# Head sums of squares of nine query and key tiles: one fp32 matmul, or two rounded passes over high and low parts

## What is computed

```python
def rms_norm_2(x, g):
    xf = x.astype(jnp.float32)
    y = xf * lax.rsqrt(jnp.mean(xf * xf, axis=-1, keepdims=True) + EPS)
    return (y * g.astype(jnp.float32)).astype(x.dtype)

    qa = apply_axial_rope_2(rms_norm_2(qa, q_gain), *rope_axial)
    ka = apply_axial_rope_2(rms_norm_2(ka, k_gain), *rope_axial)
```

## Time and profile before

| | |
|---|---|
| median of 3 runs | 2500.09 us (2498.11 to 2503.15) |
| the profiled execution, its own time | 2499.82 us |
| its span, first to last instruction | 2497.6 us |
| PE busy | 2438.6 us (98%) |
| POOL busy | 1639.5 us (66%) |
| DVE busy | 1101.5 us (44%) |
| ACT busy | 668.8 us (27%) |
| mean granted TensorE clock | 0.996 |

### The profile page before, as it was taken

The page is one execution under the profiler, slowest core; times in us unless marked ns, Lnnn a source line. Parts: engine busy times, 40 slices in busy tenths (PEclk is TensorE's granted clock), DMA queues, the critical chain, the costliest instruction groups (busy, mean ns, idle before and its releaser), DMA issues.

```text
span 2497.6 us, 32448 instructions
## 1 busy us (share of the span) xinstructions
PE 2438.6 (98%) x11606; PEld 1976.9 (79%) x11606; DVE 1101.5 (44%) x1465; ACT 668.8 (27%) x1252; POOL 1639.5 (66%) x1431
## 2 busy tenths in 40 slices
PE   7999999999999999999999999999999999999998
PEld 4886678888888887778888888888888787788886
DVE  4454654454333227865333223333226666433311
ACT  4264521112111106652111101111112774211100
POOL 3554856666666776546666776667777775666775
PEclk9999999999999999999999999999999999999999
DMA  6314533233232332003232332333333222232332
GB/s 267 114 59 145 173 114 98 95 96 98 92 101 92 104 107 87 28 13 109 92 101 92 101 109 94 100 93 100 101 104 110 80 74 65 85 100 93 101 101 84
DMA packets 68802, 248.03 MB, mean 99 GB/s; under 512 B 7408, under 2 KB 9968, under 8 KB 68080
## 3 DMA queue, kind: packets, MB, share of 16 engines
q1 hardware_dynamic: 63808, 232.81, 29.4%
q10 hardware_dynamic: 4912, 14.12, 1.5%
HBM read 244.80 MB, written 2.10 MB: 99 GB/s over the span
## 4 chain that ended last, share of the span: by engine, by line
PE 92%; DVE 3%; ACT 2%; issue 1%; POOL 1%; DMA 1%; DVEq 0%; ACTq 0%; POOLq 0%
PE pb L541 72%; PE pb L1098 4%; PE pb L1038 2%; PE pb L806 2%; PE pb L962 2%; PE pb L550 1%; PE pb L740 1%; PE pb L709 1%; PE pb L1081 1%; PE pb L1066 1%; PE pb L1054 1%; PE pb L944 1%; ACT tb L1345 1%; PE pb L928 1%; PE pb L691 1%
## 5 line engine op out<-in xcount | busy, mean ns | idle before, releaser
L541 PE MATMUL pb<-ar,w_hi 128*128 128x512 f32 x5312 | 1644.8, 391 | 3.6 <-DVE ar L1911 2.7
L541 PEld LDWEIGHTS pb<-ar,w_hi 128*128 128x128 f32 x5312 | 995.1, 188 | 222.1 <-issue 8.1
L541 PE MATMUL pb<-ar,w_lo 128*128 128x512 f32 x2656 | 1034.2, 389 | 0.0
L394 POOL TENSOR_TENSOR w_lo<-raw,w_hi 128x1024 fp32r<-128x1024 f32 x380 | 952.1, 2505 | 31.7
L541 PEld LDWEIGHTS pb<-ar,w_lo 128*128 128x128 f32 x2656 | 499.0, 188 | 103.9
L391 POOL TENSOR_TENSOR still<-still 128x1 f32<-128x1 f32 x393 | 81.3, 207 | 693.4 <-PE pb L541 550.8
L392 POOL TENSOR_SCALAR w_hi<-raw 128x1024 fp32r<-128x1024 f32 x380 | 403.7, 1062 | 0.0
L1986 DVE TENSOR_TENSOR tb<-pb,nb 128x512 f32<-128x512 f32 x88 | 60.9, 692 | 400.8 <-PE pb L541 400.8
L1992 DVE TENSOR_TENSOR ar<-tb,ar 128x512 f32 x88 | 156.2, 1775 | 90.9 <-ACT ar L1416 90.9
L1416 ACT ACTIVATE ar<-tb 128x512 f32 x88 | 55.7, 633 | 512.8 <-DVE tb L1989 512.8
L1893 DVE SCALAR_TENSOR_TENSOR x<-pb,x 128x512 f32<-128x512 f32 x48 | 36.2, 755 | 344.2 <-PE pb L541 339.8
(11 more groups left out here) (257 smaller groups left out, 2396.9 us busy)
## 6 DMA issues: line engine op xcount, KB each, us to landing
raw<-wstream SPq DMA_DIRECT2D x428, 512.0 KB, 3.6
raw<-wstream SPq DMA_DIRECT2D x4, 1024.0 KB, 10.7
x<-xt ACTq DMA_DIRECT2D x2, 2048.0 KB, 9.8
tb<-wstream SPq DMA_DIRECT2D x2, 1024.0 KB, 11.7
rt<-wstream SPq DMA_DIRECT2D x2, 1024.0 KB, 11.9
out<-x ACTq DMA_DIRECT2D x8, 256.0 KB, 2.2
rt<-nbias ACTq DMA_DIRECT2D x4, 384.0 KB, 3.8
nb<-nbias ACTq DMA_DIRECT2D x4, 384.0 KB, 3.6
```

The costliest lines, as they stand in the source:

```text
L394: pool.tensor_tensor(lo, src, hi.bitcast(F32), ALU.subtract).then_inc(s_split, 1)
L541: mm = pe.matmul(pb[:, bank, :], weights(a, n, t)[:, k * P:(k + 1) * P], rhs(b, k0 + k), start=(first and k == 0 and i == 0), stop=(last a ...
```

## The change

For calls 8 to 16 (`SPLIT_CALLS`), the fp32 matmul over the squares becomes two fp32r passes. ACT squares the tile twice: into PSUM bank 5 in fp32, and into SBUF as the rounded high part. DVE subtracts the one from the other, which is the low part (`square_lo`). PE multiplies a rounded copy of `bones` with both parts and adds them up. The copy of `bones` is made twice by ACT, once ahead of either stage. PE now waits for the low part (`s_sqlo`). In stage even2 the sum of squares of norm n3, which uses bank 5 too, waits for call 12's low part, and the value projection waits for call 11's before its tile t=4.

```diff
+        SPLIT_CALLS = tuple(c for c in range(8, len(CALLS)) if CALLS[c][2] is not None)
+
+        def squares(c, part):
+            o = (12288 if c < 12 else 22528) + TOK * part
+            return ar[:, o:o + TOK]
+
+        def bones_r(c):
+            o = (12288 if c < 12 else 22528) + 2 * TOK
+            return ar[:, o:o + P]
...
-                if gain is not None:
+                if c in SPLIT_CALLS:
+                    pe.wait_ge(s_bones, 1 if c < 12 else 2)
+                    pe.wait_ge(s_sqlo, SPLIT_CALLS.index(c) + 1)
+                    pe.matmul(pb[:, 6, :], bones_r(c), squares(c, 0), start=True, stop=False)
+                    pe.matmul(pb[:, 6, :], bones_r(c), squares(c, 1), start=False, stop=True).then_inc(s_qss, 1)
+                elif gain is not None:
...
+                        if k == 0 and t == 4:
+                            pe.wait_ge(s_sqlo, 4)
...
+                        pe.wait_ge(s_sqlo, SPLIT_CALLS.index(12) + 1)
                         sum_squares("n3", 5)
...
             def qk_square(c, bank):
                 n = CALLS[c][5]
+                if c in SPLIT_CALLS:
+                    i = SPLIT_CALLS.index(c)
+                    if i > 0:
+                        act.wait_ge(s_sqlo, i)
+                        act.wait_ge(s_qss, calls_before(c, "norm"))
+                    act.activation(pb[:, 5, :], pb[:, bank, :], ACT.Square).then_inc(s_sqp, 1)
+                    act.activation(squares(c, 0), pb[:, bank, :], ACT.Square).then_inc(s_qsq, 1)
+                    return
...
+            act.activation(bones_r(8), bones, ACT.Copy).then_inc(s_bones, 1)
...
+                if m == 0:
+                    act.activation(bones_r(12), bones, ACT.Copy).then_inc(s_bones, 1)
...
+            def square_lo(c):
+
+                i = SPLIT_CALLS.index(c)
+                dve.wait_ge(s_sqp, i + 1)
+                dve.wait_ge(s_qsq, calls_before(c, "norm") + 1)
+                dve.tensor_tensor(squares(c, 1), pb[:, 5, :], squares(c, 0).bitcast(F32), ALU.subtract)\
+                    .then_inc(s_sqlo, 1)
...
             for m in range(4):
+                square_lo(8 + m)
                 qk_gain(8 + m, m % 4)
...
                 else:
+                    if c in SPLIT_CALLS:
+                        square_lo(c)
                     qk_gain(c, m % 4)
```

More of the change, by code:

```diff
@@ L261, in build @@
         s_qcx = sem("k_ctx_evacuated")
+        s_sqp, s_sqlo, s_bones = sem("squares_in_psum"), sem("squares_lo"), sem("head_ones_rounded")
         s_gains = sem("gains_by_partition")
```

## The result

The changed kernel takes 2507.33 us (median of 8 runs, 2505.7 to 2511.37), the kernel before, in the runs beside it, 2500.49 us (8 runs, 2498.11 to 2503.15). The ratio is 1.0029, with a 95% interval of 1.002 to 1.0037: slower by about 7 us. Forecast were 2506.7 us and a range of 2500.3 to 2511. The profiled execution took 2507.55 us with a span of 2505.5 us, 7.9 us more than before.

The account below looks back on a forecast made before the run. PE, busy for 98% of the span, was taken as the bound. New waits 8.5 us less 3.6 us saved give 4.9 us, plus 1.7 us for one clock fall: 6.6 us longer, 2506.7 us, range 2500.3 to 2511.

Parts of the forecast that it names:

- The saving: Nine sums of squares on PE: two passes at 0.46 us replace an fp32 sum at 0.86 us, 3.6 us back.
- the best case: Whole kernel with all waits gone: 3.6 us saved, 2496.5 us; chance of faster 0.04.
- Call 8: PE asks at 167.50, but DVE is in call 7's product until 169.87; PE stands for 3.1 us.
- Calls 9 to 11: No wait at 9, at most 0.1 us at 10; value projection waits 1.0 us for call 11's gain, not 0.5.
- Calls 12 to 16: Stage even2: no wait at 12, then PE waits 1.4, 3.1, 0.5 and 0.1 us at calls 13 to 16.
- the way out that the prediction named: Call 14: if call 13's product (the text says call 14's) came before POOL's L394, the wait would be 1 us.
- The clock: Behind the two long waits, calls 8 and 14: one fall of PE's clock taken as the middle, 1.7 us lost.
- The two rows of before: Earlier trace: PE idle 2.92 us before 352.19 and 2.68 us before 2127.39, both followed by slow passes.
- The sum: Whole kernel: waits 8.5 us less 3.6 us is 4.9 us, plus one clock fall 1.7 us: 6.6 us longer.
- The low parts didn't come in time: Rival at calls 8 and 14: low parts in time, so not slower; 2500.3 us, or 2496.5 without waits; chance 0.17.
- The two passes did what the change says: Rival at the nine sums: two passes cost what the fp32 sum costs, 10.2 us longer, 2510.3 us; chance 0.05.
- The lag in stretch E: Rival in stage even2: ACT and DVE stay behind, lag carried on, 9.6 us longer, 2509.7 us; chance 0.07.

Follow-up runs that it names:

- The run with the sum in PSUM: Changed kernel, but DVE writes the sum ahead of the last product into the rotated tile's PSUM bank instead of SBUF; one execution, 2508.62 us.
- the run without the waits: Changed kernel without low parts: ACT squares once, PE multiplies the rounded part twice, no subtraction on DVE; 2497.99 us, ratio 0.9985.

## Why the prediction was right

**The saving.** 0.40 us a call was right for the pair itself, and in the changed kernel all nine are won, if the waits are counted apart from them, as the prediction does. What was too high is the best case, 3.6 us with all waits gone: without the low parts, the kernel gained 3.0 us, and in stretch E 0.9 us of 2.3, since PE then waits for the squares.

**Call 8.** Forecast were 3.1 us of standing, measured were 2.91 us in the trace, 3.07 us with the overlap. Cause and place are shown: the low part goes ahead of call 7's product, and the wait is 0.78 us.

**Calls 9 to 11.** No wait at 9, under 0.1 us at 10, and 0.95 us for call 11's gain instead of 0.46: as forecast.

**Calls 12 to 16.** Forecast 1.4, 3.1, 0.5 and 0.1 us; measured, with the overlap, 1.34, 3.35, 0 and 0.53 us. The step to call 14 had a wrong detail. It had call 13's product held and then the table's scaling pass; the product just got through and the scaling was held. The time comes out alike, since either is held until POOL's operation ends. The run with the sum in PSUM shows which one counted: the product's hold gone, the wait stayed. So the way out that the prediction named, a product ahead of L394 and a wait of 1 us, was no way out: the product did come ahead, and the wait was 3.2 us. Call 15's wait was forecast too high and call 16's too low; the two nearly cancel.

**The clock.** One fall in two was the guess, 1.7 us the price, and 1.3 us what it cost in the profile; over all profiles one fall cost 1.3 to 2.8 us. Behind call 8's wait of 2.9 us the clock fell in two of five profiles, behind call 14's wait of 2.9 to 3.2 us in four of five. The two rows of before, which both showed a fall, would have made both sure. That a wait of the same length, behind the same work, was followed by a fall in one execution and by none in another fits the rule of the Trainium skill (TensorE: Matmul & The Clock Gate, Part 1) that the gate's stretches run freely; no run here tests it further. The prediction took neither all nor nothing, and with that the sum was right by its middle, not by knowledge of the single case.

**The sum.** 4.9 + 1.7 = 6.6 us were forecast, 6.8 us measured between the medians. In the profiles the two stretches give 6.6 us. The terms, read from the changed kernel's trace with the overlap: new waits 8.6 us (forecast 8.5), saving 3.6 us, clock 1.3 us (forecast 1.7), in sum 6.3 us. Luck had a part in it: calls 15 and 16 cancel, the profiled execution had exactly one fall, and the same kernel, measured again, was 10.5 us above the kernel before.

**The rivals.** The low parts didn't come in time. The two passes did what the change says. That they do so at 0.46 us is shown by the run without the waits. The lag in stretch E isn't carried on: behind E the changed kernel is 0.4 us ahead, not behind.

## What to carry to other kernels

Before an operation on the busiest engine is made cheaper by work on idle ones, find the place of that work in their order and what stands ahead of it; an engine that is busy for 44% of the span was late just where the new operand was needed. Keep what the busiest engine waits for ahead of what nobody waits for, but check every reader of the work that is moved back, since a hold moves with it. And a saving is only won in full where the loop through the other engines has slack, which can be tried cheaply by a kernel that has the saving and leaves out the work behind it.

## What the runs showed that I had not expected

In the kernel before, ten of the 17 last products (L1768) meet no splitting operation of POOL's and take 0.69 us, or 0.42 us with 256 columns. The other seven, and one scaling of the table, run into one; those of 512 columns end 0.53 to 0.55 us behind its end, the one of 256 columns 0.28 us behind. That is 0.14 us less than they take alone, so they seem to do nothing until POOL is done (an estimate from these rows). The same operation with one input from PSUM takes 0.69 us in 13 of 13 cases. POOL's memset doesn't hold DVE: in the kernel before, L1775 ran in 0.68 us inside it. Here is the memset, and the operation inside it, from the two engines' timelines:

```profile
950.32 0.96 POOL L473 MEMSET ar<- 128x1024 f32 x1
```

```profile
950.49 0.68 DVE L1775 TENSOR_TENSOR ar<-tb,ar 128x512 fp32r<-128x512 f32 x1
```

That is what the Trainium skill (SBUF — State Buffer, SBUF: two separate sides) says of the port pair that both engines share: an operation of DVE with two SBUF inputs and one of GpSimd that reads SBUF lock each other out. The trace agrees, and for POOL's side too: in the changed kernel its L404 took 2.93 us at 959.86, where call 13's product had begun before it, and 2.40 us at 969.56, with no such product at its start.

The clock also falls where PE never stands for more than 1.6 us: in the first attention, between 290 and 310 us, in seven of the fourteen profiles taken, the changed kernel's among them and the kernel before's not. From the changed kernel:

```profile
290.00:300.00 10.00, 8.05 (x55) 6.56 (x51) 8.66 (x15) 6.71 (x16) 8.45 (x11) 0.85 0.32 107
```

It comes with some executions and not with others. With the falls behind long waits it may make up a part of the 3 to 6 us by which executions of one kernel differ, as those with the longer times show the lower mean clock (the changed kernel's fastest had 0.995 at 2505.7 us, its slowest 0.992 and 0.991 at 2511.4 and 2511.3 us). A single profile of either kernel is therefore no measure of a change of this size; the waits in it are.
